# Two fused transformer blocks on one core: weight projections as three float32r products of split weights, in half panels, instead of one float32 product

## What is computed

```python
# first block (w_in: 1024 x 5120)
h = rms_norm(x, g) * (1 + scale) + shift          # shift, scale, gate = c @ w_ada + b_ada
u, zp, q, k, v, za, merge_gates = split(h @ w_in)
y_attn = attention(rope(q), rope(k), v)           # 8 heads of 64, causal
merged = gate_p * (pool(u) * silu(zp) @ w_pool_up) + gate_a * (y_attn * silu(za) @ w_attn_up)
x = rms_norm(x + gate * (merged @ w_out)) * g_final
# second block
h = modulate(rms_norm(x))                         # shift, scale, gate from c_2 @ w_ada_2
r_q, r_k, r_v, r_g, n_q, kv..., n_gate = split(h @ w_in_2)   # 1024 x 3352
mix = concat(retention(r_q, r_k, r_v, r_g), nsa(n_q, kv..., n_gate)) @ w_out_2
x = x + gate * mix
h = modulate(rms_norm(x))
x = x + gate2 * peer(h @ w_peer_q, subkeys, w_down, w_up)    # 16384 experts, top 16 of 8 heads
return rms_norm(x)
```

## Time and profile before

| | |
|---|---|
| median of 3 runs | 1410.75 us (1407.55 to 1412.11) |
| the profiled execution, its own time | 1412.18 us |
| its span in the trace | 1409.6 us |
| granted TensorE clock, mean | 0.96 of full speed |
| TensorE busy | 1324.0 us (94%) |
| VectorE, ScalarE, GpSimd busy | 862.3, 466.2, 336.1 us |
| bytes by DMA | 244.19 MB, mean 173 GB/s |

### The profile page before, as it was taken

The page is one execution under the profiler, slowest core; times in us unless marked ns, Lnnn a source line. Parts: engine busy times, 40 slices in busy tenths (PEclk is TensorE's granted clock), DMA queues, the critical chain, the costliest instruction groups (busy, mean ns, idle before and its releaser), DMA issues.

```text
span 1409.6 us, 17917 instructions
## 1 busy us (share of the span) xinstructions
PE 1324.0 (94%) x7022; PEld 1040.5 (74%) x7022; DVE 862.3 (61%) x1594; ACT 466.2 (33%) x893; POOL 336.1 (24%) x150
## 2 busy tenths in 40 slices
PE   5899999969989797999898999999999999999997
PEld 1444555437745556899898999999998888888885
DVE  3545542244363622079998399999986666666666
ACT  1012110001112311054443544443345555555553
POOL 0000000000000000058989766666640000000000
PEclk9999999978688989999999999999999999999999
DMA  9876662226253112235565544444446666666664
GB/s 378 339 284 275 264 265 87 93 91 237 111 222 135 62 60 81 98 112 178 161 180 154 175 137 148 136 139 147 135 150 194 194 194 194 194 195 194 192 193 152
DMA packets 54514, 244.19 MB, mean 173 GB/s; under 512 B 6944, under 2 KB 7328, under 8 KB 42016
## 3 DMA queue, kind: packets, MB, share of 16 engines
q1 hardware_dynamic: 54000, 242.34, 49.8%
q10 hardware_dynamic: 432, 0.72, 0.2%
HBM read 240.94 MB, written 2.10 MB: 172 GB/s over the span
## 4 chain that ended last, share of the span: by engine, by line
PE 87%; DVE 6%; POOL 3%; issue 1%; ACT 1%; DMA 1%; SPq 0%; POOLq 0%; DVEq 0%
PE bank L779 21%; PE bank L1112 8%; PE bank L1079 8%; PE bank L1115 8%; PE bank L1118 8%; PE bank L1076 8%; PE bank L1075 8%; PE bank L1088 4%; PE bank L1046 4%; POOL split_r L554 3%; PE bank L968 2%; PE bank L788 1%; DVE tab L1192 1%; PE bank L771 1%; PE bank L889 1%
## 5 line engine op out<-in xcount | busy, mean ns | idle before, releaser
L554 POOL TENSOR_TENSOR split_r<-ring,split_r 128x1024 fp32r<-128x1024 f32 x128 | 326.3, 2553 | 182.8 <-ACT split_r L711 182.2
L711 ACT ACTIVATE split_r<-ring 128x1024 fp32r<-128x1024 f32 x256 | 269.2, 1052 | 245.8 <-PE bank L1079 245.8
L779 PE MATMUL bank<-G 128*128 128x512 f32 (+1 forms) x608 | 270.2, 604 | 6.5 <-DVE G L1300 4.1
L1075 PE MATMUL bank<-h_high_r,split_r 128*128 128x256 f32 x1024 | 256.2, 288 | 1.7 <-ACT split_r L711 1.7
L1076 PE MATMUL bank<-h_low_r,split_r 128*128 128x256 f32 x1024 | 250.8, 283 | 0.0
L779 PEld LDWEIGHTS bank<-G 128*128 128x128 f32 x608 | 118.1, 197 | 149.2 <-issue 147.7
L1568 DVE TENSOR_TENSOR split_r<-ring,split_r 128x1024 fp32r<-128x1024 f32 x128 | 156.9, 1225 | 66.6 <-ACT split_r L711 66.6
L1075 PEld LDWEIGHTS bank<-h_high_r,split_r 128*128 128x128 f32 x1024 | 195.9, 191 | 1.9 <-issue 1.9
L1076 PEld LDWEIGHTS bank<-h_low_r,split_r 128*128 128x128 f32 x1024 | 196.4, 192 | 0.0
L1079 PE MATMUL bank<-h_high_r,split_r 128*128 128x256 f32 x1024 | 144.9, 284 | 9.3 <-POOL split_r L554 9.3
L1079 PEld LDWEIGHTS bank<-h_high_r,split_r 128*128 128x128 f32 x1024 | 131.9, 192 | 11.5 <-POOL split_r L554 11.5
(11 more groups left out here) (231 smaller groups left out, 1365.4 us busy)
## 6 DMA issues: line engine op xcount, KB each, us to landing
ring<-in_down SPq DMA_DIRECT2D x128, 512.0 KB, 3.5
ring<-in_up SPq DMA_DIRECT2D x128, 512.0 KB, 3.5
G<-in_ada SPq DMA_DIRECT2D x36, 1024.0 KB, 11.1
G<-in_in SPq DMA_DIRECT2D x32, 1024.0 KB, 7.1
G<-in_out SPq DMA_DIRECT2D x8, 1024.0 KB, 8.3
G<-in_wq SPq DMA_DIRECT2D x8, 1024.0 KB, 7.1
G<-in_poolup SPq DMA_DIRECT2D x2, 1024.0 KB, 6.1
G<-in_attnup SPq DMA_DIRECT2D x2, 1024.0 KB, 10.1
```

What stands on the lines that cost most here:

```text
L554: pool.tensor_tensor(wsplit[:, j % SPLIT, 1, :], raw[:, j % RAW, :], wsplit[:, j % SPLIT, 0, :].bitcast(F32), ALU.subtract).then_inc(low_r ...
L711: nc.scalar.activation(wsplit[:, n % SPLIT, 0, :], raw[:, n % RAW, :], ACT.Copy).then_inc(high_ready, 1)
L779: ins = mm(bank[:, 0:cols], lhs[c], rhs[c], start=(c == 0), stop=(c == n - 1))
L1075: mm(o, w[0][:, c, :], h_high[:, c, :], start=(c == 0), stop=False)
```

## The change

**Half panels.** The unit of the stream is half a panel, 1 MB. There are eight slots of 1 MB. Half panels of projections take a pair of slots: the raw weights come into the first, ScalarE writes their high part into the second (`panel_split`), and the low part overwrites the raw weights. Slots 0 to 5 make three such pairs; slots 6 and 7 are left to the sums of `ada`. In what follows w0, w1, w2, ... are the half panels of the projections in their order: w0, w1 are `in1` 2; w2, w3 `in1` 3; w4, w5 `in1` 4; w6 to w19 those beside the heads; w20 to w23 `poolup` and `attnup`; w24 to w27 `out1`; w28, w29 `in2` 5; w30, w31 `in2b`; w32, w33 `in2` 4; w34 to w41 `in2` 0 to 3; w42 to w45 `out2`; w46 to w53 `wq`.

**Three products.** Each half panel is 24 float32r matmuls of 512 columns instead of 8 float32 ones: 16 with the high weights, then 8 with the low ones, over both token tiles. The left operands (`hT`, `upT`, `mT`) are split as well, by ScalarE and VectorE. All projections of tile t go to bank t, where four banks were taken in turn.

**Who makes the low part.** VectorE for w0 to w29 and for w46, w47, one instruction of 2048 columns each (`panel_rest`, placed at the step of the half panel before it). GpSimd makes the others, in pieces of 512, and none in the first block.

**Sums.** 17 panels of `ada` are now summed by VectorE, in halves placed at the steps that `SUM_AT` names, most with their running sum in PSUM; one is left on TensorE. Smaller edits: the keys of the second block are transposed without the doubling copy by GpSimd, the pool stage and the output projection are laced into the heads, the loads of the gate rows come later in the stream.

The core of the diff:

```diff
-PANEL = C * 512
-SLOTS = 4
+HALF = C * 256
+SLOTS = 8
...
+SUM_AT = [0, 1, 3, 5, 6, 8, 10, 11, 13, 15, 16, 18, 21, 22, 24, 25, 28, 29, 30, 31, 32, 33, 33.5, 33.5, 46, 47, 49, 51]
...
+    at, w = [], -1
+    for n, s in enumerate(weights):
+        w += s[3] == "pe"
+        out.append(s)
+        while len(at) < len(sums) and w >= (0 if len(at) < 2 else SUM_AT[len(at) - 2] + 2) and s[3] == "pe":
+            out.append(sums[len(at)])
+            at.append(n)
+    return out + [("subkeys", None, 0, "raw")]
...
+            at[n] = 6 + turn % 2
+            turn += 1
+        else:
+            at[n] = 2 * pairs.pop(0)
+            pairs.append(at[n] // 2)
+        used = [at[n]] if user == "dve" or n < SLOTS else [at[n], at[n] + 1]
+        before[n] = [last[k] for k in used if k in last]
+        for k in used:
...
+LOW_BY_VECTOR = SPLITS[:SPLITS.index(AT["in2b", None, 0])] + [AT["wq", 0, 0], AT["wq", 0, 1]]
...
+        users = [step_of[m] for m in BEFORE[n] if m in step_of] + ([step_of[SPLITS[w - 2]]] if w >= 2 else [])
+        latest = max([latest] + users)
+        at.setdefault(latest, []).append(n)
...
+    if s[0] in ("proj", "wout"):
+        bank = s[3]
...
+                for b in BEFORE[n]:
+                    half_used(sp, b)
...
+                if n == AT["in1", IN1[2], 1]:
+                    sp.dma_start(gateA, d["gate1"].partition_broadcast(P)).then_inc(gate_in, 16)
...
+                        for c in range(0, words, PIECE):
+                            part = slice(c, min(c + PIECE, words))
+                            ins = pool.tensor_tensor(lo[:, part], raw_[:, part], hi[:, part], ALU.subtract)
+                        ins.then_inc(panel_low, 1)
...
+            def panel_split(n):
+
+                words = WORDS.get(STREAM[n][0], HALF)
+                src = wait_half(act, n)[:, 0:words]
+                nc.scalar.activation(slot_r[SLOT_OF[n] + 1][:, 0:words], src, ACT.Copy).then_inc(panel_high, 1)
...
+                for n in HIGH_AT.get(k, ()):
+                    if n != SPLITS[0]:
+                        panel_split(n)
...
+                pe_.wait_ge(panel_high, SPLITS.index(n) + 1)
+                for part in (x_high_, x_low_):
+                    for s, o, tok in outs:
+                        for c in range(4):
+                            mm(o, part[:, chunks + c, tok], hi[:, c, :], start=(first and part is x_high_ and c == 0), stop=False)
+                wait_low(pe_, n)
+                for s, o, tok in outs:
+                    for c in range(4):
+                        ins = mm(o, x_high_[:, chunks + c, tok], lo[:, c, :], start=False, stop=(last and c == 3))
+                    if last:
+                        bank_full(ins, s)
+                if not last:
...
+                    col_ = cc[:, 4 * half + c:4 * half + c + 1]
+                    if half == 0 and c == 0:
+                        ins = ts(a, w[:, 0, :], col_, None, ALU.mult)
+                    else:
+                        ins = stt(out=total if half == 1 and c == 3 else a, in0=w[:, c, :], scalar=col_, in1=a,
+                                  op0=ALU.mult, op1=ALU.add)
...
+                    dve.wait_ge(gate_in, 48)
...
+                lo, raw_, hi = low_half(dve, n)
+                tt(lo, raw_, hi, ALU.subtract).then_inc(panel_low_dve, 1)
```

More of the change, by code:

```diff
@@ L64 @@
[L64 to L84, removed]
@@ new lines, with stream @@
+ADA += [("ada2", i) for i in (2, 3, 0, 1, 4, 5, 8, 9, 6, 7, 10, 11)]
+FIRST = 3
+SUM_AT = [0, 1, 3, 5, 6, 8, 10, 11, 13, 15, 16, 18, 21, 22, 24, 25, 28, 29, 30, 31, 32, 33, 33.5, 33.5, 46, 47, 49, 51]
+def stream():
+    halves = lambda panels, user: [(name, i, h, user) for name, i in panels for h in range(2)]
+    out = halves([ADA[0]], "dve") + halves([("ada1", 0)], "row") + halves(ADA[1:FIRST], "dve")
+    early = [("in1", i) for i in IN1] + [("poolup", None), ("attnup", None), ("out1", 0), ("out1", 1)]
+    weights = halves(early + [("in2", 5), ("in2b", None), ("in2", 4)], "pe") + halves([("cmpk", None), ("cmpv", None)], "raw")
+    weights += halves([("in2", i) for i in range(4)] + [("out2", 0), ("out2", 1)] + [("wq", p) for p in range(4)], "pe")
+    sums = halves(ADA[FIRST:], "dve")
+    at, w = [], -1
[6 more added lines that the diff above has]
+    return out + [("subkeys", None, 0, "raw")]
@@ new lines, with half, transposed @@
+SLOT_OF, BEFORE = slots()
+LOADS = {n: sum(SLOT_OF[m] == SLOT_OF[n] for m in range(n + 1)) for n in range(len(STREAM))}
+GATE2 = [("ada2", 4), ("ada2", 5)]
+def steps():
+    out, early = [], [0]
+    def half(name, i, h):
+        out.append(("half", name, i, h))
+        w = early[0]
+        early[0] += 1
+        for k in range(len(SUM_AT)):
+            if SUM_AT[k] == w:
+                out.append(("sum", FIRST + k // 2, k % 2))
+            if k % 2 and int(SUM_AT[k] + 1) == w and ADA[FIRST + k // 2] not in GATE2:
+                out.append(("ada", *ADA[FIRST + k // 2]))
+        if name in ("poolup", "attnup"):
+            out.extend(("up", name, t, h) for t in range(NT))
+        elif h == 1 and name in ("in1", "in2", "in2b"):
+            out.extend(("proj", name, i, t) for t in range(NT))
+        elif h == 1 and name in ("out1", "out2"):
+            out.extend(("wout", int(name[3]) - 1, i, t) for t in range(NT))
+        elif h == 1:
+            out.extend(("peerq", 2 * i + k) for k in range(2))
+    def panel(name, i):
+        for h in range(2):
+            half(name, i, h)
+    def transposed(b):
+        out.extend(("xT", b, t, h) for h in range(2) for t in range(NT))
@@ L119, in heads @@
                 out.append(("pv", first + i - 2))
-    ada_after(AT[("in1", 2)], ada)
-    out.extend(("xT", 0, t, half) for t in range(NT) for half in range(2))
+    both = lambda kind, *rest: [(kind, *rest, k) for k in range(2)]
+    transposed(0)
     panel("in1", 2)
@@ new lines, in power @@
+            def power(k):
+                pool.wait_ge(var_ready, k)
+                pool.tensor_tensor(rstd, ss, half_neg[:, 0:2], ALU.pow).then_inc(rstd_ready, 1)
+            halves = lambda *panels: [(name, i, h) for name, i in panels for h in range(2)]
+            low(halves(*[("in1", i) for i in IN1], ("poolup", None), ("attnup", None), ("out1", 0), ("out1", 1)))
+            power(2)
+            power(3)
+            low(halves(("in2b", None), ("in2", 4), *[("in2", i) for i in range(4)]) + [("out2", 0, 0)])
```

689 lines of the change are left out of this document (398 added, 291 removed).

## The result

The changed kernel takes 1454.64 us (median of 4 runs, 1450.05 to 1459.02), the kernel before on the same chips 1409.15 (1406.96 to 1412.11): a ratio of 1.032, 95% interval 1.028 to 1.036. It is slower by 3.2%, 50 us above the 1405 predicted and 23 above the range.

A forecast was written before the change was run, and what follows sets the result against it. TensorE, busy 94% of the span, was taken as the bound; of 78 us its products would save, all but 5 go into waits: 1409.6 - 7.5 (stages) + 3 (clock) = 1405.1, stated as 1405 us, range 1381 to 1432.

The forecast's parts named there:

- The load of w(v+2) is issued at t, lands at t+4.9.: First-block heads: load, high part and two evacuations end at t+8.0, against t+7.8 for product and head.
- 6 + 5 + 5 = 16 us: Heads 0 to 6: lateness at w6, w10 and w16, where an `ada` load waits for its half sum ahead of weights.
- The sums as work that hides: VectorE's half sums, 2.9 us each, were charged only at stages where they would be late, as in the heads.
- `in2` 5, `in2b`, `in2` 4, +10.5: Stage after the first norm: 40.7 us becomes 51.2, with gaps of 5 and 5.7 us for evacuations.
- This is where the one bank a tile costs most: Stage `in2` 5, `in2b`, `in2` 4: single banks leave evacuations uncovered, with gaps of 5 and 5.7 us.
- The gate row, +7: In `in1` 2, 3, 4: VectorE waits at w2 for a gate row loaded behind w5's load, +7 us.
- Heads 8 to 15, -12.9, and 16 to 23, -7.8: Second-block heads: 78.3 us becomes 65.4 as products shorten and sums leave VectorE's chain; 82.4 with `out2` falls by 7.8.
- The clock, +3: Some fourteen further waits of 2 us or more; two taken in full at 1.6 us each, all would be +22.
- rival 1: Whole kernel: the clock falls in every wait, 1.6 us each, fourteen 22 us, giving 1425 us; chance 0.30.
- The 2.6 us for a cold clock: Allowance for slow products at the start of the stage from `in2` 5 and of the queries.
- Rival 2: Loads come early enough: heads at 13.5 us without 18 us of late ones, no gate wait, 1380 us; chance 0.15.
- Rival 3: GpSimd too slow for the second block: eight close low parts each 1.5 us later, +12, 1417 us; chance 0.13.

The follow-up runs named there:

- experiment 1: Changed kernel with ScalarE's high part of a half panel made behind the evacuations of the panel that ends, not ahead: 1436.3 us, ratio 1.018.
- experiment 7: Changed kernel with the first block's `ada` loads (from the fourth matrix on) issued by GpSimd, not SP: 1434.8 us, ratio 1.018.
- the four edits: Changed kernel with high part behind evacuations, gate rows behind tables, first-block `ada` loads on GpSimd's queue, two pairs of banks: 1392.7 us, ratio 0.987.
- experiment 5: Changed kernel without the vector instructions of the column sums from the fourth `ada` matrix on, their loads kept: 1417.5 us, ratio 1.006.
- experiment 9: Changed kernel with `in1` 3, `in2b`, `out1` 1 and the second half of `attnup` on banks 2 and 3: 1441.2 us, ratio 1.021.
- experiment 2: Changed kernel with the three gate rows loaded behind the tables (behind w1's load), not behind w5's: 1446.6 us, ratio 1.024.
- experiment 16: Changed kernel with VectorE making the low parts of the second block and queries too, GpSimd none: 1458.6 us, ratio 1.035.
- experiment 8: Changed kernel with high part behind evacuations, gate rows behind tables, and first-block `ada` loads on GpSimd's queue: 1407.6 us, ratio 0.998.
- the run with ten fillings: Changed kernel with extra float32r matmuls, their result overwritten, put into ten of its pauses: 1449.3 us, ratio 1.028.

## Why the prediction was wrong

The waits that the prediction named were there; it had their sizes wrong. The stages lost 48.3 us more than forecast: 17.6 in heads 8 to 23, 12.3 from `in2` 5 to the compression, 8.2 in heads 0 to 6, the other 10.2 in small parts. What failed, by the prediction's own steps:

- **"The load of w(v+2) is issued at t, lands at t+4.9."** Right for a load alone (4.85 at 182.41), wrong for the heads that decide: 7.0 to 7.4 us in the late ones. I had charged the queue with 6 + 5 + 5 = 16 us and left the landing at 4.9 everywhere, though the earlier trace rows held the 7.1. The pauses were 8.9, 6.3 and 6.5 us. The three late loads are 6.7 us later than 4.9 each, and the heads' stage was mis-sized by 8.2 us. The wait for ScalarE's high part was named rightly (18 us, experiment 1), and so was the queue (20 us, experiment 7).
- **The sums as work that hides.** The prediction asked of the half sums where they would be late, stage by stage, and named some 25 us (16 in the heads, 3.4 and 5.7 behind norm 1, where the gates and small sums are in them). On the chain that ended last the instructions of sums grew by 33 us, from 16 to 49; with the four edits they are 11. How much of the 52 us that the changed kernel gains without sums the kernel before would gain too, no run shows. Between norm 1 and head 8, where I had put 9.1 us and nothing in the compression, their vector work alone is 15 us (11 and 4.5, experiment 5).
- **`in2` 5, `in2b`, `in2` 4, +10.5**: the gaps of 5 and 5.7 us were 5.9 and 7.9, and both products behind them began at the half clock (granted 0.50 from 340.75 to 344.82 and from 358.13 to 361.20), which cost 1.7 and 2.2 us. "This is where the one bank a tile costs most" held: the stage is 14 us shorter with the second pair (experiment 9), and 11 us shorter without the vector work of the sums (experiment 5). No run has both.
- **The gate row, +7**: 8.2 us for the last row, 8 us by experiment 2. Right.
- **Heads 8 to 15, -12.9, and 16 to 23, -7.8**: the largest miss, -3.3 and +0.2. The products did save what they should: TensorE is busy 8.7 and 9.1 us less (64.4 for 73.1, 64.9 for 74.0), and the forecast had 9.4 each. What failed is the wait. The prediction had the idle time shrink by 3.5 us in the first eight heads and grow by 1.5 in the others; it grew by 5.4 and 9.3. The clock is not the difference in heads 8 to 15: there the first products are as slow in the kernel before, 9.80 and 8.78 us for 7.06. Of the idle time a part is GpSimd, which I gave 5.1 us a half panel (5.2 measured, right) and no effect on VectorE: with no low part on it heads 8 to 15 are 4.4 us shorter and the whole 6 to 10 (experiment 16). Both tiles of `in2` 0 and `in2` 1 are now rotated one behind the other with no product beside them (pauses of 4.3 and 3.9 us), where before one tile's rotation lay under the next tile's product; that this is the remaining cause was not shown by a run, only that neither the banks nor the place of `in2` 3 are. The rest stays open.
- **The clock, +3**, with 22 as the other bound: too low, and by how much stays open. A fall costs a product 1.9 to 3.1 us in most places and not 1.6 (the first sixteen matmuls take from 5.59 us at 161.06 to 6.70 at 254.23, for 3.63); the first sixteen matmuls in heads 0 to 6 alone took 7.8 us too long. The mean clock over the first 300 us, 0.87, is below the 0.9 that was to show rival 1. Against rival 1 as the main cause stand two things. Once three waits were taken away, the slow products of those heads went with them (experiment 8): there the clock's loss followed from waits that have other causes. And pauses filled gave back 5 us of 15 and 0 of 13. But only some pauses were filled, and at a price, so rival 1, which I held for the second likeliest, is not excluded as a part of the loss; it had the direction right. The 2.6 us for a cold clock at `in2` 5 and at the queries, and the 2 behind the gate, were estimates without a row: by the starts in the timeline the first sixteen matmuls at 319.18 took 6.5 us for 3.8, the first sixteen of the queries (256 columns, 584.37) took 3.55 for 1.92, and behind the gate, at 88.30, 4.3 for 3.8.
- **Rival 2** (1380 us, loads early enough) describes what heads 0 to 6 do once experiments 1, 2 and 7 are made: seven panels in 91.1 us, where it had 7 x 13.5.
- **Rival 3**: no run shows its 1.5 us for each of eight low parts. GpSimd took 4.9 to 5.3 us for one of 2048 columns in the changed kernel between 344 and 560 us (6.0 at 587.60), and no wait of TensorE in the first 650 us is put down to it. What the runs do show beside it is VectorE's slower rotations and scaling (experiment 16).
- **Slips in the sum**, of no weight: the heads give 112.9 us, +1.2 and not +1.6; `in1` 2 to 4 give 6 + 7 + 2 - 9.1 = +5.9 and not +6.1. Of the -12.9 for heads 8 to 15 the products explain 9.4; the 3.5 for sums that leave the chain are not worked out.

The products themselves came out as computed. As I read it, the error was to sum small waits one by one, each with its cover as the kernel before had it, while all covers shrank by the same change.

## What to carry to other kernels

A product that gets faster takes away cover from everything laid under it; before its gain is counted, the work of each other engine and the bytes per product have to be set against the new length, not the old. Look for what stands ahead of the critical item in an in-order queue (an `ada` load ahead of a weights' load, a high part ahead of an evacuation, a gate that waits for its row ahead of low parts and an evacuation): here three such places, each a few lines, gave back 46 us and a second pair of banks 13 to 15 more, and the kernel is then 1.3% faster than the one before. Where leaving work out is the experiment, leave it out of both kernels: a gain in one of them says nothing of what the change did. And the engine or bank named in a wait need not be its cause: try the next item in that engine's queue.

## What the runs showed of the hardware

- VectorE's rotations with two sources in SBUF (128x256) slow down while GpSimd subtracts beside them: 0.42 us with no low part on GpSimd, 0.77 in the mean and 1.48 at most with it; those with a source in PSUM stay at 0.415. Of the changed kernel's six of L1372, the two at 1.48 us (433.05 and 453.13) lie inside GpSimd's subtractions (429.09 to 434.24 and 451.64 to 456.96), and the four at 0.42 (375.38, 377.63, 436.36, 457.17) outside all of them; the one from PSUM at 431.56 (L1370), inside the first, takes 0.41. The scaling of the scores (L1492, 128x256), with one tensor in SBUF, does so too: 0.41 and 0.53 in the mean, 1.42 at most (of two that stand at 426.30 to 427.82, GpSimd subtracting from 422.44 to 427.41).
- Pauses filled with matmuls raised the mean granted clock from 0.925 to 0.942 and brought about 5 us, and from 0.938 to 0.961 and brought none, the price of the fillings included. What filling gave back is less than what it took off the slow products' own excess (5 of 15 us, 0 of 13).
- In the run with ten fillings a pause of 1.74 us left the product behind it, at 61.60, at the full clock (2.08 us for eight matmuls, granted 1.00), and one of 2.20 us, at 125.40, did not (3.65 us, granted 0.53); but neither did one of 1.46 us, at 552.04 (3.65 us, granted 0.51), with short pieces of work and small pauses ahead of it. The last pause alone does not tell at which clock a product starts.
